# Attention heads 0 to 2: the four logit tiles in one run in four banks, the transposes of the probabilities in pairs

## The chip, the cores and the metric

The kernel runs on one core of one Trainium2 chip. The metric is the device time of one execution in microseconds (us). The engines are named as in the profile: PE is TensorE (matmuls and transposes), PEld its weight loads, DVE is VectorE, ACT is ScalarE, POOL is GpSimd, SP is SyncE, which issues the DMAs.

## The reference

One decoder layer over 512 tokens of width 1024. The part around the change is its sparse attention, four heads of width 128:

```python
(hq, hf, hi, hg, aq, ak, av, iq, ik, iw) = jnp.split(h @ w_in[layer], split_points, axis=-1)
o_hg = hgrn2_mixer(hq, hf, hi, hg, ...)          
q = partial_rope(q.reshape(B, T, ATT_HEADS, ATT_HEAD_DIM), positions)
k = partial_rope(k.reshape(B, T, ATT_HEADS, ATT_HEAD_DIM), positions)
score = jnp.einsum('bqh,bqhs->bqs', wi, jax.nn.relu(s))     # indexer, causal
_, idx = lax.top_k(score, topk)                             # 128 keys for each query
logits = jnp.einsum('bqhd,bqkhd->bhqk', qb, ks) * scale
p = jax.nn.softmax(jnp.where(valid, logits, -inf))
o = jnp.einsum('bhqk,bqkhd->bqhd', p, vs)
y = jnp.concatenate([o_hg, o_att], axis=-1) @ w_out[layer]
```

Before it stand the modulated norm and the input projection, beside it the gated linear recurrence (HGRN2), and behind it the output projection and the SwiGLU feed-forward layer. The kernel doesn't gather the selected keys: it adds a bias of about -1e30 to the logits of the keys that were not selected.

## The kernel before

The program is written engine by engine; the order on every engine is the order of the code, and semaphores tie the engines together. Weights and activations are split in a high and a low part, and each product with a weight is three matmuls (high by high, high by low, low by high). `w_raw` is the weight that a DMA loads, ACT makes `w_hi` of it (`split_hi`, L527), and DVE `w_lo` (`split_lo`, L1013). There are eight PSUM banks of 128 x 512, `ps[0]` to `ps[7]`.

**PE** (from L2007). `att_body(h, first)` treats attention head h; h = 0 is written out (`first`), h = 1 and 2 are a loop on the engine, and head 3 is code of its own (from L2073), between pieces of the output projection. While head h is attended, PE projects the q, k and v of head h + 1: 24 steps of three matmuls (`fill`, `att_project`, L1671), eight steps each for q, k and v, into banks 1, 0 and 1. Between them stand, for the four row tiles t = 0 to 3 of head h (128 queries each, t + 1 blocks of 128 keys):

- `logits(h, t, bank)`, L2009: one fp32 matmul of 128 x 128(t + 1), which the profile shows as two instructions. The logits 0 and 1 go to banks 2 and 3, the logits 2 and 3 to banks 2 and 3 again, once DVE has read them (`te.wait_ge(lg_ok, ...)`).
- `turn_v`, L2014: the four transposes of v into bank 6.
- `turn_probs(h, t, bank)`, L2022: t + 1 transposes of the probabilities into bank 4 or 5, after `p_ok`, which DVE raises.
- `values(h, t, 7)`, L2029: the product with the values, into bank 7.

The order is: steps 0 to 4, wait for the rotation (`a_rope`), logits 0 and 1, `turn_v`, (head 0: two steps), logits 2 and 3, steps up to 7, then three steps ahead of each `turn_probs`, four steps, `values`.

**ACT** (`att_body`, L793 to L826) goes in this order for each head: it waits for `turn_v` (`v_mm`) and copies bank 6 to `av_tok` (L802); exponentials of tiles 0 and 1 (L813); the copy of the next head's q out of its bank (`att_raw`, L718) and `split_hi`; the exponential of tile 2; the transposed probabilities of tile 0 out of their bank (`put_pt`, L806); the exponential of tile 3; `put_pt(1)`; `att_raw` of k; `put_pt(2)`, `put_pt(3)`; `att_raw` of v.

**DVE** (`att_body`, L1396 to L1456) goes in this order: `split_lo`; for each tile the logits plus bias out of the bank into `probs[t]` with the row maximum (L1414), the negated maximum (L1418), and then `normalise(t - 1)` (L1402, L1404), which waits for the exponential of tile t - 1; after tile 2 two `add_sum` (L1104, work for later modulation) and a `split_lo`; `normalise(3)`; two more `add_sum`, `split_lo`, and the rotation of the next head's q and k (`att_rotate`, L1386 to L1391), which raises `a_rope`; the copy of bank 7 (L1455).

Names in the trace: `res` holds aq, ak, av, av_tok, the probabilities and their transposes; `mx` and `nmx` are row maxima, `rs` and `ri` row sums and their inverses. `oln_ok` counts ACT's reads of bank 4 at the end of the recurrence's heads.

Of the kernel before, what the change touches and what calls it, by code (L numbers as in the profile page):

```python
# [7 lines left out]
P = 128  # L8
D_MODEL = 1024
SEQ = 512  # L10
HG_HEADS = 4
ATT_HEADS = 4
# [8 lines left out]
TT = SEQ // P  # L21
# [48 lines left out]
def build(nc, x, c, positions, w_ada, b_ada, norm_post_mix, norm_post_ffn, w_in, w_out, w_ffn_in, w_ffn_out, small_rows,  # L70
# [5 lines left out]
    with ctx:  # L76
# [78 lines left out]
        probs = [part(res, p_off[t], P * (t + 1)) for t in range(TT)]  # L155
# [31 lines left out]
        ps = [ctx.enter_context(nc.psum_tensor(f"ps{b}", [P, SEQ], f32)) for b in range(8)]  # L187
# [334 lines left out]
        def _(sc):  # L522
# [272 lines left out]
            def att_body(h, last):  # L795
                if last:
                    for k in range(4):
                        split_x_hi(k)
                        if k in (1, 2):
                            split_hi(1 + k, U_OUT[1 + k], G_OUT)  # L800
                sc.wait_ge(v_mm, h + 1)
                sc.activation(av_tok, ps[6][:, :], ACT.Copy).then_inc(v_ok, 1)  # L802

                def put_pt(t):
                    sc.wait_ge(pt_mm, h * 4 + (t + 1))
                    sc.activation(pt.rearrange("p (s t) -> p s t", s=TT)[:, 0:t + 1, t * P:(t + 1) * P],  # L806
                                  ps[7 - t % 2 if last else 4 + t % 2][:, 0:P * (t + 1)].rearrange(
                                      "p (s t) -> p s t", s=t + 1),
                                  ACT.Copy).then_inc(pt_ok, 1)

                for t in range(TT):
                    sc.wait_ge(nm_ok, h * 4 + (t + 1))
                    sc.activation(probs[t], probs[t], ACT.Exp, bias=nmx[:, t:t + 1], scale=float(HEAD ** -0.5),  # L813
                                  accum_out=rs[:, t:t + 1]).then_inc(exp_ok, 1)
                    if t == 1 and not last:
                        att_raw(h + 1, (0,))
                    if t >= 2:
                        put_pt(t - 2)
                    if last and t == 2:
                        sc.activation(ones_r[:, :], ones[:, :], ACT.Copy).then_inc(ones_ok, 1)  # L820
                        sc.wait_ge(sum_used, KT)
                        sc.activation(first_hi[:, :], sum_gate_mix, ACT.Copy).then_inc(gate_hi_ok, 1)
                if not last:
                    att_raw(h + 1, (1,))
                put_pt(2)
                put_pt(3)  # L826
                if not last:
                    att_raw(h + 1, (2,))
# [172 lines left out]
        def _(ve):  # L1001
            V = nc.vector
# [390 lines left out]
            def att_body(h, first, last):  # L1393
                sums = ((0, 1, 2, 3), range(4, 10), range(10, 14), (14, 15))[h]
                if first:
                    ve.wait_ge(sin_ok, 4)  # L1396
                    att_rotate(0)
                    ve.wait_ge(top_rep, HG_HEADS * 12)

                def normalise(t):  # L1400
                    ve.wait_ge(exp_ok, h * 4 + (t + 1))
                    V.reciprocal(ri[:, t:t + 1], rs[:, t:t + 1]).then_inc(ri_ok, 1)  # L1402
                    ve.wait_ge(ri_ok, h * 4 + (t + 1))
                    V.tensor_scalar(probs[t], probs[t], ri[:, t:t + 1], None, ALU.mult).then_inc(p_ok, 1)  # L1404

                if not (first or last):
                    split_lo(h * 3 + (G_ATT + 4), 1)
                for t in range(TT):
                    if first and t:
                        V.tensor_scalar(bias_t[t], sc_t[t], TAKEN / 2, NEG, ALU.is_gt, ALU.mult).then_inc(bias_ok, 1)  # L1410
                        ve.wait_ge(bias_ok, t)

                    ve.wait_ge(lg_mm, h * 4 + (t + 1))
                    V.tensor_tensor_reduce(out=probs[t], in0=ps[(4 if last else 2) + t % 2][:, 0:P * (t + 1)],  # L1414
                                           in1=bias_t[t], scale=1.0, scalar=TAKEN, op0=ALU.add, op1=ALU.max,
                                           accum_out=mx[:, t:t + 1]).then_inc(lg_ok, 1)
                    ve.wait_ge(lg_ok, h * 4 + (t + 1))
                    V.tensor_scalar(nmx[:, t:t + 1], mx[:, t:t + 1], float(-HEAD ** -0.5), None,  # L1418
                                    ALU.mult).then_inc(nm_ok, 1)
                    if t:  # L1420
                        normalise(t - 1)
                    if first and t == 1:
                        split_lo(G_ATT + 4, 1)
                    if last and t < 3:
                        split_x_lo(t + 1)
                        split_lo(G_OUT + 1 + t, 1 + t)
                    if not last and t == 2:
                        add_sum(sums[0])
                        add_sum(sums[1])
                        split_lo(h * 3 + (G_ATT + 5), 2)  # L1430
                normalise(TT - 1)
                if first:
                    head_tail(HG_HEADS - 1)
                if not last:
                    add_sum(sums[2])
                    add_sum(sums[3])
                    split_lo(h * 3 + (G_ATT + 6), 0)
                    att_rotate(h + 1)
                    for i in sums[4:]:
                        add_sum(i)  # L1440
                if h == ATT_HEADS - 2:
                    split_x_lo(0)
                if last:
                    ve.wait_ge(gate_hi_ok, 1)
                    V.tensor_tensor(first_lo[:, :], sum_gate_mix, first_hi[:, :].bitcast(f32),
                                    ALU.subtract).then_inc(gate_lo_ok, 1)
                    add_sum(sums[0])
                    add_sum(sums[1])
                    ve.wait_ge(post_loaded, 16)
                    for b in range(2):  # L1450
                        ve.wait_ge(gate_mm, b + 1)
                        V.tensor_tensor(gate_mix[:, b * SEQ:(b + 1) * SEQ], ps[(5, 7)[b]][:, :],
                                        gate_mix[:, b * SEQ:(b + 1) * SEQ], ALU.mult).then_inc(gate_ok, 1)
                ve.wait_ge(pv_mm, h * 4 + 4)
                V.tensor_copy(mix[:, (HG_HEADS + h) * SEQ:(HG_HEADS + h + 1) * SEQ],  # L1455
                              ps[4 if last else 7][:, :]).then_inc(att_out, 1)  # L1456
# [205 lines left out]
        def _(te):  # L1662
# [187 lines left out]
            for unit in (2, 3, 4):  # L1850
                k, first = START_TILES[unit][0] - 1, 4 * int(unit == 2)
# [152 lines left out]
            hg_body(HG_HEADS - 1, True)  # L2004

            def logits(h, t, bank):
                if t >= 2:  # L2007
                    te.wait_ge(lg_ok, h * 4 + (t - 1))
                mm(ps[bank][:, 0:P * (t + 1)], aq[:, t * P:(t + 1) * P], ak[:, 0:P * (t + 1)], start=True,  # L2009
                   stop=True).then_inc(lg_mm, 1)  # L2010
# [6 lines left out]
            def turn_probs(h, t, bank):  # L2017
                te.wait_ge(p_ok, h * 4 + (t + 1))
                if t >= 2:
                    te.wait_ge(pt_ok, h * 4 + (t - 1))  # L2020
                for s in range(t + 1):
                    last_mm = nc.tensor.transpose(ps[bank][:, s * P:(s + 1) * P], probs[t][:, s * P:(s + 1) * P],  # L2022
                                                  ident[:, :])
                last_mm.then_inc(pt_mm, 1)
# [8 lines left out]
            def att_body(h, first):  # L2033
                def fill(start, end):

                    att_project(h + 1, start, end)

                if not first:
                    te.wait_ge(v_ok, h)
                te.wait_ge(a_raw, h * 3 + 3)  # L2040
                fill(0, 5)
                te.wait_ge(a_rope, h * 2 + 2)
                logits(h, 0, 2)
                logits(h, 1, 3)
                turn_v()
                if first:
                    fill(5, 7)
                logits(h, 2, 2)
                logits(h, 3, 3)
                fill(7 if first else 5, 8)  # L2050
                for t in range(TT):
                    fill(8 + 3 * t, 11 + 3 * t)
                    if t == 1:
                        te.wait_ge(v_ok, h + 1)
                    turn_probs(h, t, 4 + t % 2)
                fill(20, 24)
                if first:
                    te.wait_ge(hg_out, HG_HEADS)
                for t in range(TT):
                    values(h, t, 7)  # L2060
# [237 lines left out]
```

## Time and profile before

| | |
|---|---|
| time, median of 3 runs | 693.54 us (693.03 to 693.98) |
| the profiled execution: its own time | 693.87 us |
| its span | 692.1 us |
| PE busy | 680.6 us, 98% of the span |
| DVE busy | 555.7 us, 80% |
| ACT busy | 334.5 us, 48% |
| DMA, mean rate | 128 GB/s |
| granted clock of PE, mean | 1.0 |

The span goes from the first to the last instruction that the profile shows; the time of the execution also holds what lies around it. Times in the views count from the span's start. A line of a timeline gives the start, the time up to the end of the last of the merged instructions, the engine, the line of the kernel, the operation and its count; what stands in square brackets is the engine's idle time ahead of it and what ended it. The attention heads 0 to 2 take the stretch from about 214 to 284 us.

### The profile page before, as it was taken

The page shows a single profiled execution, that of the slowest core. Times are in us where ns is not written, and L with a number is a line of the kernel's source. Part 1 is how long each engine was busy: PE and PEld are TensorE (multiplying, and loading weights), DVE is VectorE, ACT ScalarE, POOL GpSimd, SP SyncE. Part 2 cuts the span into 40 slices and gives each one's busy share as a digit, 9 for nine tenths or more (in the row PEclk, how much of TensorE's full clock was granted, in tenths as well). Part 3 has the DMA queues.
Part 4 walks back from the last instruction along what each step waited for, and adds up shares of the span by engine and source line. Part 5 has one row for each costly group of instructions (what it writes and reads, how often), then busy time and mean ns, then how long its engine had stood idle before and what let it go on. Part 6 is the DMA issues. An engine that isn't in the chain of part 4 may idle for free.

```text
span 692.1 us, 12998 instructions
## 1 busy us (share of the span) xinstructions
PE 680.6 (98%) x4640; PEld 567.9 (82%) x4640; DVE 555.7 (80%) x938; ACT 334.5 (48%) x569; POOL 135.1 (20%) x109
## 2 busy tenths in 40 slices
PE   7999999999999999999999999999999999999996
PEld 6566677777777878888788999999999998888885
DVE  3777999898898988988977799999999985344444
ACT  7357653545445344545753455555556551121123
POOL 4000000000000000000005567666766700000000
PEclk9999999999999999999999999999999999999999
DMA  9963222232224656568163255344433443322202
GB/s 274 357 207 95 61 63 62 75 107 61 62 62 119 217 183 217 179 230 254 31 183 91 71 145 149 115 130 130 131 110 114 122 131 126 109 92 91 61 10 112
DMA packets 97707, 88.92 MB, mean 128 GB/s; under 512 B 2735, under 2 KB 86787, under 8 KB 97670
## 3 DMA queue, kind: packets, MB, share of 16 engines
q1 hardware_dynamic: 97670, 88.44, 42.1%
q8 instruction: 21, 0.34, 0.2%
q14 instruction: 16, 0.13, 0.1%
HBM read 86.33 MB, written 2.10 MB: 128 GB/s over the span
## 4 chain that ended last, share of the span: by engine, by line
PE 62%; DVE 4%; issue 1%; ACT 0%; DVEq 0%; ACTq 0%
PE ps L2196 26%; PE ps L1690 17%; PE ps L1671 7%; PE ps L1708 6%; DVE rope L1104 1%; PE ps L2009 1%; DVE w_lo L1013 1%; PE ps L2029 1%; PE ps L2167 1%; PE ps L2174 1%; PE ps L1729 1%; PE ps L2169 1%; DVE act L1386 0%; DVE res L1391 0%; DVE act L1389 0%
## 5 line engine op out<-in xcount | busy, mean ns | idle before, releaser
L1671 PE MATMUL ps<-h_hl,w_hi 128*128 128x512 f32 x544 | 176.5, 405 | 0.0
L527 ACT ACTIVATE w_hi<-w_raw 128x1024 fp32r<-128x1024 f32 (+1 forms) x72 | 72.7, 1015 | 98.7 <-PE ps L1690 83.9
L1671 PEld LDWEIGHTS ps<-h_hl,w_hi 128*128 128x128 f32 x544 | 97.7, 188 | 24.6 <-issue 5.5
L1671 PE MATMUL ps<-h_hl,w_lo 128*128 128x512 f32 x272 | 106.6, 392 | 0.0
L2196 PE MATMUL ps<-h_hl,w_hi 128*128 128x256 f32 x576 | 104.5, 283 | 0.0
L2196 PEld LDWEIGHTS ps<-h_hl,w_hi 128*128 128x128 f32 x576 | 90.0, 192 | 0.2
L1013 DVE TENSOR_TENSOR w_lo<-w_raw,w_hi 128x1024 fp32r<-128x1024 f32 (+1 forms) x72 | 84.9, 1184 | 5.6 <-ACT w_hi L527 5.1
L1690 PE MATMUL ps<-w_hi,ht_hl 128*128 128x512 f32 x288 | 88.9, 389 | 0.0
L2196 PE MATMUL ps<-h_hl,w_lo 128*128 128x256 f32 x288 | 81.5, 283 | 0.0
L2196 PE MATMUL ps<-ht_hl,w_hi 128*128 128x256 f32 x432 | 78.5, 283 | 0.0
L2196 PEld LDWEIGHTS ps<-ht_hl,w_hi 128*128 128x128 f32 x432 | 67.4, 192 | 0.0
L1690 PEld LDWEIGHTS ps<-w_hi,ht_hl 128*128 128x128 f32 x288 | 54.1, 188 | 11.2
L2196 PE MATMUL ps<-ht_hl,w_lo 128*128 128x256 f32 x216 | 61.1, 283 | 0.0
L1671 PEld LDWEIGHTS ps<-h_hl,w_lo 128*128 128x128 f32 x272 | 51.1, 188 | 11.3
L1690 PE MATMUL ps<-w_lo,ht_hl 128*128 128x512 f32 x144 | 56.0, 389 | 0.0
L2196 PEld LDWEIGHTS ps<-h_hl,w_lo 128*128 128x128 f32 x288 | 55.3, 192 | 0.0
L1541 DVE TENSOR_TENSOR w_lo<-mix,w_hi 128x1024 fp32r<-128x1024 f32 x36 | 50.5, 1403 | 5.4 <-ACT w_hi L924 5.2
L1541 DVE TENSOR_TENSOR w_lo<-w_raw,w_hi 128x1024 fp32r<-128x1024 f32 (+1 forms) x36 | 53.2, 1478 | 0.0
L1550 DVE CAST ht_hl<-act 128x512 fp32r (+1 forms) x22 | 9.4, 426 | 53.7 <-PE ps L1690 53.2
L924 ACT ACTIVATE w_hi<-mix 128x1024 fp32r<-128x1024 f32 x36 | 38.0, 1056 | 22.8 <-PE ps L2196 18.9
L503 POOL TENSOR_TENSOR mix<-w_raw 128x512 f32<-128x512 f32 x18 | 23.8, 1324 | 117.1 <-DMA w_raw<-in_w_ffn_in 73.5
L491 POOL MEMSET res<- 128x1024 f32 x1 | 1.0, 962 | 230.1 <-DVE mix L1455 230.1
(310 smaller groups left out, 1260.2 us busy)
## 6 DMA issues: line engine op xcount, KB each, us to landing
w_raw<-in_w_ffn_in SPq DMA_DIRECT2D x44, 512.0 KB, 4.6
w_raw<-in_w_in SPq DMA_DIRECT2D x28, 512.0 KB, 4.0
w_raw<-in_w_ffn_out SPq DMA_DIRECT2D x22, 512.0 KB, 3.6
act<-in_w_ada SPq DMA_DIRECT2D x12, 512.0 KB, 8.4
adaw<-in_w_ada SPq DMA_DIRECT2D x6, 1024.0 KB, 5.2
act<-in_w_ada SPq DMA_DIRECT2D x6, 1024.0 KB, 5.2
res<-in_x SPq DMA_DIRECT2D x8, 512.0 KB, 5.6
w_raw<-in_w_out SPq DMA_DIRECT2D x8, 512.0 KB, 5.4
```

The source lines that it names most:

```text
L503: pool.tensor_tensor(s1, up_w[:, 0:QUART], up_w[:, QUART:2 * QUART], ALU.add).then_inc(s_ok, 1)
L527: sc.activation(w_hi[slot][:, 0:n], w_raw[slot][:, 0:n], ACT.Copy).then_inc(hi_ok, 1)
L924: sc.activation(w_hi[u][:, 0:src.shape[1]], src, ACT.Copy).then_inc(hi_ok, 1)
L1013: V.tensor_tensor(w_lo[slot][:, 0:n], w_raw[slot][:, 0:n], w_hi[slot][:, 0:n].bitcast(f32), ALU.subtract).then_inc(lo_ok, 1)
L1104: V.scalar_tensor_tensor(out=total, in0=w, scalar=silu, in1=total, op0=ALU.mult, op1=ALU.add).then_inc(sum_used, 1)
L1541: V.tensor_tensor(w_lo[u][:, 0:n], src, w_hi[u][:, 0:n].bitcast(f32), ALU.subtract).then_inc(lo_ok, 1)
L1550: V.tensor_copy(ht_hi[:, at], act[:, ds(k * SEQ, SEQ)]).then_inc(xs_hi, 1)
L1671: last = mm(ps[bank][0:rows, :], a, b, start=(k == 0 and n == 0), stop=(k == KT - 1 and n == 2))
L1690: last = mm(ps[2 * t + b][:, :], a, w, start=(first and n == 0), stop=False)
L1708: last = mm(ps[2 * t + b][:, :], a, w, start=False, stop=(n == 3 and m == 2))
L1729: return nc.tensor.transpose(ps[k][:, t * P:(t + 1) * P], xn[:, t * D_MODEL + k * P:t * D_MODEL + (k + 1) * P], ident[:, :])
L2196: last_mm = mm(ps[bank][:, 0:HALF], a, b, start=(start and k == 0 and n == 0), stop=(k == 3 and n == 2), skip_group_check=not start)
```

## The change

The four logit tiles of a head come right behind one another, into banks 2, 3, 4 and 5, without a wait for DVE between them, and `turn_v` comes behind them. The steps 5 to 12 follow in one run, then the transposes of the probabilities of tiles 0 and 1, the steps 13 to 18, the transposes of tiles 2 and 3, and the steps 19 to 23. The transposes go to banks 4, 2, 3 and 4. Ahead of those of tile 0 PE waits until DVE has read the logits of tile 2 out of bank 4; in head 0 it waits, ahead of the logits, for ACT's last read of bank 4 (`oln_ok`). Head 3 keeps its order and banks. DVE and ACT change only the bank that they read.

```diff
@@ -804,7 +804,7 @@
                 def put_pt(t):
                     sc.wait_ge(pt_mm, h * 4 + (t + 1))
                     sc.activation(pt.rearrange("p (s t) -> p s t", s=TT)[:, 0:t + 1, t * P:(t + 1) * P],
-                                  ps[7 - t % 2 if last else 4 + t % 2][:, 0:P * (t + 1)].rearrange(
+                                  ps[7 - t % 2 if last else (4, 2, 3, 4)[t]][:, 0:P * (t + 1)].rearrange(
                                       "p (s t) -> p s t", s=t + 1),
                                   ACT.Copy).then_inc(pt_ok, 1)
 
@@ -1411,7 +1411,7 @@
                         ve.wait_ge(bias_ok, t)
 
                     ve.wait_ge(lg_mm, h * 4 + (t + 1))
-                    V.tensor_tensor_reduce(out=probs[t], in0=ps[(4 if last else 2) + t % 2][:, 0:P * (t + 1)],
+                    V.tensor_tensor_reduce(out=probs[t], in0=ps[4 + t % 2 if last else 2 + t][:, 0:P * (t + 1)],
                                            in1=bias_t[t], scale=1.0, scalar=TAKEN, op0=ALU.add, op1=ALU.max,
                                            accum_out=mx[:, t:t + 1]).then_inc(lg_ok, 1)
                     ve.wait_ge(lg_ok, h * 4 + (t + 1))
@@ -2004,7 +2004,7 @@
             hg_body(HG_HEADS - 1, True)
 
             def logits(h, t, bank):
-                if t >= 2:
+                if bank > 3 and isinstance(h, int) and h == ATT_HEADS - 1 and t >= 2:
                     te.wait_ge(lg_ok, h * 4 + (t - 1))
                 mm(ps[bank][:, 0:P * (t + 1)], aq[:, t * P:(t + 1) * P], ak[:, 0:P * (t + 1)], start=True,
                    stop=True).then_inc(lg_mm, 1)
@@ -2040,20 +2040,20 @@
                 te.wait_ge(a_raw, h * 3 + 3)
                 fill(0, 5)
                 te.wait_ge(a_rope, h * 2 + 2)
-                logits(h, 0, 2)
-                logits(h, 1, 3)
+                if first:
+                    te.wait_ge(oln_ok, HG_HEADS)
+                for t in range(TT):
+                    logits(h, t, 2 + t)
                 turn_v()
-                if first:
-                    fill(5, 7)
-                logits(h, 2, 2)
-                logits(h, 3, 3)
-                fill(7 if first else 5, 8)
-                for t in range(TT):
-                    fill(8 + 3 * t, 11 + 3 * t)
-                    if t == 1:
-                        te.wait_ge(v_ok, h + 1)
-                    turn_probs(h, t, 4 + t % 2)
-                fill(20, 24)
+                fill(5, 13)
+                te.wait_ge(lg_ok, h * 4 + 3)
+                turn_probs(h, 0, 4)
+                te.wait_ge(v_ok, h + 1)
+                turn_probs(h, 1, 2)
+                fill(13, 19)
+                turn_probs(h, 2, 3)
+                turn_probs(h, 3, 4)
+                fill(19, 24)
                 if first:
                     te.wait_ge(hg_out, HG_HEADS)
                 for t in range(TT):
```

The first place is PE in the loop of heads 1 and 2, from the end of the first five steps (L1671) on: logits (L2009) and transposes of v (L2014), with the semaphores that each row waits for. Before:

```order
L2042 ISA
L2009 MATMUL ps<-res 128x128 [waits a_rope]
L2009 MATMUL ps<-res 128x256
L2014 MATMUL ps<-ident,res 128x128 x4
L2008 ISA
L2009 MATMUL ps<-res 128x384 [waits lg_ok]
L2008 REGISTER_ALU
L2009 MATMUL ps<-res 128x512 [waits lg_ok]
L1671 MATMUL ps<-h_hl,w_hi 128x512 x2
```

And now:

```order
L2042 ISA
L2009 MATMUL ps<-res 128x128 [waits a_rope]
L2009 MATMUL ps<-res 128x256
L2009 MATMUL ps<-res 128x384
L2009 MATMUL ps<-res 128x512
L2014 MATMUL ps<-ident,res 128x128 x4
L1671 MATMUL ps<-h_hl,w_hi 128x512 x2
```

The logits of 384 and 512 columns have moved ahead of the four transposes of v, and their two waits for DVE are gone.

The second place is PE in the same loop, at the transposes of the probabilities (L2022) of tiles 0 and 1, as it is now:

```order
L2049 ISA
L2018 REGISTER_ALU [waits lg_ok]
L2022 MATMUL ps<-ident,res 128x128 [waits p_ok]
L2018 REGISTER_ALU [waits v_ok]
L2022 MATMUL ps<-ident,res 128x128 [waits p_ok]
L2022 MATMUL ps<-ident,res 128x128
L1671 MATMUL ps<-h_hl,w_hi 128x512 x2
```

Three steps stood between the first of these transposes and the other two; those steps are now split between the places ahead of the pair and behind it.

The third place is ACT in head 0, whose order is the same before and after: the copy of the transposed v (L802) stands ahead of the first exponential (L813).

```order
L802 ACTIVATE res<-ps 128x512 [waits v_mm]
L813 ACTIVATE res,rs<-res,nmx 128x128 [waits nm_ok]
L813 ACTIVATE res,rs<-res,nmx 128x256 [waits nm_ok]
L718 ACTIVATE res<-ps 128x512 [waits group_done]
L527 ACTIVATE w_hi<-w_raw 128x1024 [waits group_done,w_loaded2]
```

Nothing moved here; ACT's copy follows wherever PE's transposes of v go.

## Rows read from the trace of the kernel before

**Rows 1.** The page of the profile: the span, busy time by engine, the chain of waits by engine.

```profile
span 692.1 us, 12998 instructions
...
PE 680.6 (98%) x4640; PEld 567.9 (82%) x4640; DVE 555.7 (80%) x938; ACT 334.5 (48%) x569; POOL 135.1 (20%) x109
...
PE 62%; DVE 4%; issue 1%; ACT 0%; DVEq 0%; ACTq 0%
```

**Rows 2.** Stretches of heads 0, 1, 2: length, busy us by engine, granted clock, DMA.

```profile
214.30:237.08 22.78, 22.78 (x115) 18.42 (x115) 20.30 (x44) 12.34 (x23) 0.00 (x0) 1.00 0.58 176
237.08:260.77 23.69, 22.98 (x117) 18.36 (x116) 21.56 (x45) 9.37 (x19) 0.00 (x0) 1.00 0.64 206
260.77:283.61 22.84, 22.70 (x118) 18.50 (x116) 20.72 (x42) 9.93 (x21) 0.00 (x0) 1.00 0.72 253
```

**Rows 3.** Timeline of PE, head 1: start, us, line, operation, [idle <-releaser].

```profile
240.35 0.39 PE L1671 MATMUL ps<-h_hl,w_lo 128*128 128x512 f32 x1
240.87 0.92 PE L2009 MATMUL ps<-res 128*128 128x128 f32 x4
241.62 0.60 PE L2014 MATMUL ps<-ident,res 128*128 128x128 f32 x4
242.81 1.77 PE L2009 MATMUL ps<-res 128*128 128x384 f32 x4 [0.58 <-DVE mx L1414]
...
244.88 0.39 PE L1671 MATMUL ps<-h_hl,w_lo 128*128 128x512 f32 x1
```

**Rows 4.** Timeline of PE, head 2, then the first logits of head 3.

```profile
264.27 0.82 PE L2009 MATMUL ps<-res 128*128 128x128 f32 x4
264.93 0.60 PE L2014 MATMUL ps<-ident,res 128*128 128x128 f32 x4
265.36 1.67 PE L2009 MATMUL ps<-res 128*128 128x384 f32 x4
266.47 1.02 PE L1671 MATMUL ps<-h_hl,w_hi 128*128 128x512 f32 x2
267.33 0.40 PE L1671 MATMUL ps<-h_hl,w_lo 128*128 128x512 f32 x1
...
281.08 2.39 PE L2029 MATMUL ps<-res 128*128 128x128 f32 x20
283.61 0.89 PE L2009 MATMUL ps<-res 128*128 128x128 f32 x4
```

**Rows 5.** Timeline of DVE, where heads 0 to 2 wait, and the last rotations.

```profile
220.40 0.16 DVE L1402 RECIPROCAL ri<-rs 128x1 f32<-128x1 f32 x1 [0.40 <-ACT res L813]
...
229.60 0.49 DVE L1404 TENSOR_SCALAR res<-res,ri 128x512 f32<-128x512 f32 x1
...
240.13 0.68 DVE L1391 TENSOR_TENSOR res<-act 32x512 f32<-32x512 f32 x1
...
243.50 0.16 DVE L1402 RECIPROCAL ri<-rs 128x1 f32<-128x1 f32 x1
...
248.27 1.23 DVE L1013 TENSOR_TENSOR w_lo<-w_raw,w_hi 128x1024 fp32r<-128x1024 f32 x1 [0.57 <-ACT w_hi L527]
...
265.60 0.15 DVE L1418 TENSOR_SCALAR nmx<-mx 128x1 f32<-128x1 f32 x1
266.57 0.17 DVE L1402 RECIPROCAL ri<-rs 128x1 f32<-128x1 f32 x1 [0.82 <-ACT res L813]
...
282.78 0.68 DVE L1391 TENSOR_TENSOR res<-act 32x512 f32<-32x512 f32 x1
```

**Rows 6.** Timeline of ACT: the copy of the values, head 2.

```profile
265.56 0.60 ACT L802 ACTIVATE res<-ps 128x512 f32<-128x512 f32 x1 [5.20 <-PE ps L2014]
```

**Rows 7.** Timeline of PE, head 0: the transposes of tile 2.

```profile
229.34 0.49 PE L2022 MATMUL ps<-ident,res 128*128 128x128 f32 x3
```

**Rows 8.** Timeline of PE at the start of the kernel: two runs of 128x128 transposes.

```profile
2.45 4.11 PE L1756 MATMUL ps<-ident 128*128 128x128 f32 x20
7.43 1.09 PE L1774 MATMUL ps<-ident,act 128*128 128x128 f32 x8 [0.87 <-DVE act L1065]
```

## The prediction

> **What bounds the kernel now.** I read the page first. PE is busy for 680.6 of 692.1 us, and the chain that ended last lies on PE for the most part [rows 1]. So the kernel is bound by PE's instructions in their order, and a change of order can gain only the time in which PE waits. The second view is the three stretches of heads 0 to 2, each from its first projection step to the next head's (the last up to head 3's first logits): 22.78, 23.69 and 22.84 us, with the same work in each [rows 2]. The reader should see that head 1 is 0.9 us longer than the other two.
>
> PE's timeline shows where. Head 1's last projection matmul starts at 240.35 and takes about 0.23, so it is through at 240.58; the logits start at 240.87, 0.29 late. The rotation on DVE ends at 240.13 + 0.68 = 240.81 and is what they wait for. The four transposes of v start at 241.62 and take 0.43 (in head 2, 265.36 - 264.93), so PE is free at 242.05, and the next logits start at 242.81: 0.76 of waiting, for DVE to read the first logits out of bank 2 [rows 3, 4, 5]. In head 2 that wait is not there: 265.36 - 264.93 is the transposes alone. But before head 3 there is one for DVE again: the values start at 281.08 and would end at 283.31 (20 instructions at about 0.11), the rotation ends at 282.78 + 0.68 = 283.46, and the logits start at 283.61 [rows 4, 5]. So DVE's rotation of the next head is the second bound here, 0.3 us behind PE.
>
> The third view is DVE's own waits. They are short, and the one that matters is at L1402, the inverse of the row sum of tile 0. It waits for ACT's first exponential: 0.40 in head 0, nothing in head 1, 0.82 in head 2 [rows 5]. ACT can't do that exponential before it has copied v (L802), since that copy stands ahead of it in its program, and the copy waits for PE's transposes of v: in head 2, PE's logits start at 264.27, the copy at 265.56, L1402 at 266.57 [rows 4, 6]. That is a chain of 2.30 us from the first logits to L1402.
>
> **The change part by part.**
>
> *The wait for DVE between the logits goes.* It is worth 0.76 in head 1, and with it goes the slower start of the matmuls behind the wait: from 242.81 to the third projection matmul at 244.88 it is 2.07, and in head 2 from 265.36 to 267.33 it is 1.97, so 0.10 more. Together 0.86 [rows 3, 4]. Heads 0 and 2 have nothing to give back here.
>
> *The work itself stays.* Logits 0 and 1 take 0.66 (264.27 to 264.93), or 0.75 behind a wait (240.87 to 241.62). Logits 2 and 3 take 1.51: the 1.97 just named less two projection matmuls of 0.23 each. The transposes of the probabilities are the same ten at about 0.11 each. That they stand in pairs saves nothing that I can price, since two and three of them in a row already cost that much each, and the edit goes at 0. The register instructions in the loop are as many as before, within one or two; also 0.
>
> *The transposes of v come 1.51 us later.* They now stand behind logits 2 and 3. This is the costly part. Before, bank 6 was complete 0.43 us after logits 1; now the 896 columns of logits 2 and 3 lie between. ACT's copy, its first exponential, L1402, and with L1402 everything behind it on DVE, come later by as much as DVE was already waiting there.
>
> Head 0: DVE waited there, so all 1.51 arrive: L1402 from 220.40 to 221.91. Nothing on DVE up to the rotation of head 1 has slack that could take it up, since its other waits there (for the exponential of tile 3, for its own semaphores) hang on DVE's own earlier work. PE has one small wait more: the transposes of tile 2 started at 229.34 and now stand behind two more steps of 0.69, so those of tile 3 could start at 229.34 + 1.38 + 0.33 = 231.05, but the probabilities of tile 3 come at 229.60 + 0.49 + 1.51 = 231.60 [rows 5, 7]. That is 0.55 of waiting, and it is hidden: the first five steps of the next head are then through at 240.58 + 0.55 = 241.13, while the rotation ends at 240.81 + 1.51 = 242.32.
>
> Head 1: the logits start at 240.87 + 1.51 = 242.38, after 1.25 us of waiting. The four logits and the transposes of v take 0.75 + 1.51 + 0.43, so PE is at its next step at 245.07. Before it was there at 244.88 - 0.46 = 244.42. PE is **0.65 late** (1.51 - 0.86). L1402 comes 2.30 + 0.09 + 1.51 after the first logits, at 246.28, where it was at 243.50: DVE is 2.78 late. At 248.27 DVE had waited 0.57 for `w_hi`, which ACT makes when PE is through with q, at +0.65; that wait goes, and 2.21 stay [rows 3, 5]. From here to the rotation for head 2 there is room: it ended about 3 us ahead of its need.
>
> Head 2: the logits start at 264.27 + 0.65 = 264.92, and L1402 at 264.92 + 2.30 + 1.51 = 268.73, against 266.57. DVE itself was ready at 265.60 + 0.15 = 265.75, with its 2.21 at 267.96, so ACT still ends the wait. DVE is **2.16 late** [rows 5]. Nothing behind it takes that up, and the rotation for head 3 ends at 283.46 + 2.16 = 285.62. PE, which with its 0.65 is through with the values at 283.96, waits 1.8 us for it: head 3's first logits start at 283.61 + 2.16 = 285.77.
>
> From there on PE is busy without a gap to the end of the head, and DVE's work and PE's are shifted alike. So the sum is 2 x 1.51 - 0.86 = **+2.16 us**. The profiled execution took 693.87, 0.33 over the median; it would be 696.0, and the median of the runs goes from 693.54 to **695.7 us**.
>
> *Bounds of the 1.51.* The nearest rows below it: from the start of logits 2 to the first projection matmul, 266.47 - 265.36 = 1.11. Above it: the whole 1.77 of the merged row of head 1 [rows 3, 4]. With 1.11 the sum is 1.36, with 1.77 it is 2.68, so 694.9 to 696.2. I keep 1.51, since it is measured where PE ran without a break.
>
> **The rivals.** A difference of 0.2%, 1.4 us, is about what a measurement of this kernel can tell from none.
>
> *A, not slower: the banks decide.* If DVE were not held by the late copy of v, only the wait for the bank would go. Price: -0.86 in head 1, of which head 3's rotation leaves as much as DVE also gains; its 0.82 of waiting in head 2 would let it gain about that. It gives 692.7 us. For it speaks the 0.76 on PE [rows 3]; against it the 0.82 and 0.40 in which DVE sat at L1402 for ACT already [rows 5]. It decides if the exponential can start ahead of the copy, which ACT's order does not allow. The Trainium skill speaks for it (Perfetto Trace Analysis, Matmuls): independent groups of matmuls should rotate through the banks, so that their evacuation overlaps the next group. By that rule alone the sum would be -0.86; this trace agrees with it for one wait of three heads.
>
> *B, half of it absorbed.* Somewhere between head 0 and head 3 DVE has slack that I don't see, about as large as the 0.57 for `w_hi` or the 0.82 at L1402. Price: 0.6 to 1.4 less, so 694.3 to 695.1. Against it: these two waits are already counted, and PE's 0.65 plus 1.51 lead to the same 2.16 in head 2 whatever head 0 does.
>
> *C, slower still: PE's clock falls while PE waits.* The granted clock is 1.00, the 2.4 GHz level, in all three heads, with waits of up to 0.76 [rows 2, 3]. The longest wait would now be 1.8 us, and the trace has none as long with work on both sides. At the start of the kernel, from 2.45 us on, 20 transposes take 4.11 us, 0.205 each; eight later ones take 1.09 us with the drain of the last, at most 0.14 each, and those of heads 1 and 2 0.11 [rows 4, 8]. Such a stretch costs 20 x 0.095 = 1.9 us, and the time is 697.6. Against it: behind the 0.87 of waiting at 7.43 the transposes ran at the fast rate. The Trainium skill has the mechanism (TensorE: Matmul & The Clock Gate, What's actually happening): an array that has been idle gets half of its pulses.
>
> **How the numbers follow.** The forecast has 0.74, its bounds being 694.9 and 696.2. A has 0.05, B 0.12, C 0.06, and 0.03 is for something not named, on either side. The range of 694.5 to 696.6 takes in the forecast's bounds with the scatter of a median of three (about 0.4), and most of B; what it leaves out is A, C and the lower end of B. Slower by over 0.2% means over 694.9: nearly all of the forecast (0.71), C, and a little of B, together 0.80. Within 0.2%: 0.17. Faster by over 0.2%, under 692.1, would need more than A gives: 0.03.
>
> **What would show it.** Right, if in the changed kernel: L1402 of head 0 waits about 1.9 us for the exponential, and L1402 of head 1 over 1 us where it waited for nothing; head 1's logits wait over 1 us for the rotation (L1391) and none for `mx`; PE waits about half a microsecond in head 0 for tile 3's probabilities; head 3's first logits start at about 285.8, after 1.8 us without work on PE, and the lengths from there to the end are unchanged. Wrong, if the copy L802 comes less than 1.3 us later against the head's first logits, if head 3's logits start before 285, if the wait for `mx` is still there, or if PE's matmuls behind the long wait take twice their time.

## The result and the profile after

| | before | changed |
|---|---|---|
| median | 693.52 us (692.86 to 695.15, 14 runs) | 695.54 us (694.75 to 697.56, 14 runs) |
| profiled execution, its span | 693.87 us, 692.1 us | 697.08 us, 695.4 us |
| head 0's first logits to head 3's first logits | 65.61 us | 67.64 us |

The ratio is 1.0029, with a 95% interval of 1.002 to 1.0037: the change makes the kernel slower by 2.02 us. The page of the changed kernel answers to [rows 1]: PE is 1.8 us busier and the span 3.3 us longer.

```profile
span 695.4 us, 12998 instructions
...
PE 682.4 (98%) x4640; PEld 569.2 (82%) x4640; DVE 555.7 (80%) x938; ACT 334.0 (48%) x569; POOL 135.1 (19%) x109
...
PE 62%; DVE 3%; issue 1%; ACT 0%; DVEq 0%; ACTq 0%
```

The profiled execution is 3.21 us slower than that of before, the median only 2.02. Most of the difference lies at the start. Head 0's first logits begin at 219.14 in the changed kernel and at 218.00 before, though nothing ahead of them was changed. The stretches of the changed kernel show a lower granted clock there; the last line is the middle stretch of before:

```profile
15.00:18.00 3.00, 2.94 (x18) 1.77 (x15) 1.67 (x5) 1.78 (x3) 0.00 (x0) 1.00 1.12 324
18.00:21.00 3.00, 3.00 (x21) 1.38 (x20) 1.70 (x3) 0.69 (x1) 0.00 (x0) 0.56 1.07 350
21.00:24.00 3.00, 3.00 (x21) 2.01 (x13) 0.32 (x2) 1.20 (x2) 0.00 (x0) 0.87 1.10 364
...
18.00:21.00 3.00, 3.00 (x26) 1.54 (x24) 1.98 (x3) 1.08 (x2) 0.00 (x0) 1.00 1.07 348
```

The columns are those of [rows 2]. Before, all three stretches read 1.00. The shift varies from one execution to the next and is no part of the change: four of the ten traces of this document have such a dip of the clock, and among them is one whose PE code is that of before (e4). So I read every time below from the head 0 logits of its own trace, and the stretch up to the first logits of head 3 is the measure for each kernel. Behind it the two kernels are alike: PE's last matmul starts 402.95 us after head 3's first logits in the changed kernel (689.73 - 286.78) and 402.92 before. The parts add up: 1.14 at the start, 2.03 in the stretch and 0.03 behind it are 3.20 us.

PE's timeline of the changed kernel, against [rows 3, 4, 7]; the first five lines are head 0 up to its values, the next three run from the end of the five projection steps to the transposes of v of head 1, the next three are head 2, and the last is the start of head 3:

```profile
219.14 2.42 PE L2009 MATMUL ps<-res 128*128 128x128 f32 x8
221.40 0.60 PE L2014 MATMUL ps<-ident,res 128*128 128x128 f32 x4
...
224.72 0.74 PE L1671 MATMUL ps<-h_hl,w_hi 128*128 128x512 f32 x2 [0.64 <-DVE w_lo L1013]
...
232.75 0.93 PE L2022 MATMUL ps<-ident,res 128*128 128x128 f32 x7
...
236.96 2.39 PE L2029 MATMUL ps<-res 128*128 128x128 f32 x20
...
242.37 0.39 PE L1671 MATMUL ps<-h_hl,w_lo 128*128 128x512 f32 x1
243.50 2.42 PE L2009 MATMUL ps<-res 128*128 128x128 f32 x8 [0.73 <-DVE res L1391]
245.76 0.60 PE L2014 MATMUL ps<-ident,res 128*128 128x128 f32 x4
...
266.00 2.32 PE L2009 MATMUL ps<-res 128*128 128x128 f32 x8
268.15 0.60 PE L2014 MATMUL ps<-ident,res 128*128 128x128 f32 x4
...
282.74 2.39 PE L2029 MATMUL ps<-res 128*128 128x128 f32 x20
286.78 0.89 PE L2009 MATMUL ps<-res 128*128 128x128 f32 x4 [1.66 <-DVE res L1391]
```

The reader should see that the wait for `mx` in head 1 is gone, and that two larger waits for the rotation (L1391) stand in its place, ahead of head 1's logits (0.73 in the brackets) and of head 3's (1.66). The brackets count from the modelled end of the matmul before. DVE's waits at L1402, against [rows 5], in heads 0, 1 and 2, and the end of the last rotation:

```profile
223.05 0.16 DVE L1402 RECIPROCAL ri<-rs 128x1 f32<-128x1 f32 x1 [1.91 <-ACT res L813]
...
247.41 0.16 DVE L1402 RECIPROCAL ri<-rs 128x1 f32<-128x1 f32 x1 [1.30 <-ACT res L813]
...
269.80 0.16 DVE L1402 RECIPROCAL ri<-rs 128x1 f32<-128x1 f32 x1 [0.83 <-ACT res L813]
...
285.96 0.68 DVE L1391 TENSOR_TENSOR res<-act 32x512 f32<-32x512 f32 x1
```

And ACT, against [rows 6]: in head 0 the copy of v and the exponential behind it.

```profile
222.03 0.60 ACT L802 ACTIVATE res<-ps 128x512 f32<-128x512 f32 x1 [3.13 <-PE ps L2014]
222.53 0.39 ACT L813 ACTIVATE res<-res,nmx 128x128 f32<-128x128 f32 x1
```

In head 0 the wait at L1402 grew from 0.40 to 1.91 us, by the 1.51 of logits 2 and 3. In head 1 there was none and now it is 1.30. In head 2 it is 0.83, about as before (0.82). There the exponential comes 2.1 us later than before, by PE's 0.59 and the 1.51, and DVE is ready for it 2.07 us later (268.81 + 0.15 - 1.14 = 267.82 against 265.75).

### The profile page after: what moved, and what is told of

The parts are those of the page before. It is cut to its first block, busy times and chain, and to the rows that moved or that the text cites. A ratio compares the mean times of both kernels' runs of the same rounds, so it can differ in the third digit from the quotient of the medians.

```text
span 695.4 us, 12998 instructions
## 1 busy us (share of the span) xinstructions
PE 682.4 (98%) x4640; PEld 569.2 (82%) x4640; DVE 555.7 (80%) x938; ACT 334.0 (48%) x569; POOL 135.1 (19%) x109
## 4 chain that ended last, share of the span: by engine, by line
PE 62%; DVE 3%; issue 1%; ACT 0%; DVEq 0%; ACTq 0%
PE ps L2196 26%; PE ps L1690 17%; PE ps L1671 7%; PE ps L1708 6%; PE ps L2009 1%; PE ps L2029 1%; PE ps L2167 1%; DVE rope L1104 1%; PE ps L2174 1%; PE ps L1729 1%; PE ps L2169 1%; DVE w_lo L1013 0%; DVE act L1386 0%; DVE res L1391 0%; DVE act L1389 0%
## 5 line engine op out<-in xcount | busy, mean ns | idle before, releaser
L1671 PE MATMUL ps<-h_hl,w_hi 128*128 128x512 f32 x544 | 174.9, 403 | 0.6 <-DVE w_lo L1013 0.6
L1671 PEld LDWEIGHTS ps<-h_hl,w_hi 128*128 128x128 f32 x544 | 97.9, 188 | 24.4 <-issue 4.0
L1671 PE MATMUL ps<-h_hl,w_lo 128*128 128x512 f32 x272 | 106.5, 392 | 0.0
L1690 PE MATMUL ps<-w_hi,ht_hl 128*128 128x512 f32 x288 | 88.8, 389 | 0.0
L1690 PEld LDWEIGHTS ps<-w_hi,ht_hl 128*128 128x128 f32 x288 | 54.1, 188 | 11.1
L1671 PEld LDWEIGHTS ps<-h_hl,w_lo 128*128 128x128 f32 x272 | 51.1, 188 | 11.3
L1690 PE MATMUL ps<-w_lo,ht_hl 128*128 128x512 f32 x144 | 56.0, 389 | 0.0
```

The lines of the kernel that those rows point to most:

```text
L1671: last = mm(ps[bank][0:rows, :], a, b, start=(k == 0 and n == 0), stop=(k == KT - 1 and n == 2))
L1690: last = mm(ps[2 * t + b][:, :], a, w, start=(first and n == 0), stop=False)
```

## The experiments

The theory: ACT's copy of v stands ahead of its first exponential, so putting logits 2 and 3 ahead of the transposes of v makes DVE late, once in head 0 and again by head 2, and head 3 waits for it. The rivals: the four banks or the pairs of transposes cost the time, or the place of the copy has no effect.

Eight kernels were run. The comparison is with before on the same chip (median 693.45 for the first four, 693.69 for the last four). The "stretch" is that from head 0's first logits to head 3's in the profiled execution.

| kernel | median us | ratio to before (95%) | stretch us |
|---|---|---|---|
| before | 693.5 to 693.7 | | 65.61 |
| changed | 695.54 | 1.0029 (1.002 to 1.0037) | 67.64 |
| e1: changed, v's transposes early | 692.41 | 0.9984 (0.9975 to 0.9993) | 64.73 |
| e2: before, v's transposes late | 698.83 | 1.008 (1.0066 to 1.0093) | 71.26 |
| e3: changed, copy of v late on ACT | 692.56 | 0.9985 (0.9976 to 0.9994) | 64.24 |
| e4: before, copy of v late on ACT | 692.90 | 0.9989 (0.998 to 0.9998) | 65.07 |
| e5: before, pairs alone | 693.47 | 0.9995 (0.9987 to 1.0004) | 65.59 |
| e6: e1 and e3 together | 692.36 | 0.9983 (0.9974 to 0.9991) | 64.22 |
| e7: changed, v's transposes later still | 697.92 | 1.0065 (1.0052 to 1.0079) | 69.04 |
| e8: e3, and the rotation earlier on DVE | 692.69 | 0.9984 (0.9975 to 0.9992) | 63.94 |

**e1, the transposes of v back between the logits.**

```diff
-                for t in range(TT):
-                    logits(h, t, 2 + t)
-                turn_v()
+                logits(h, 0, 2)
+                logits(h, 1, 3)
+                turn_v()
+                logits(h, 2, 4)
+                logits(h, 3, 5)
                 fill(5, 13)
```

> The changed kernel with the transposes of v back between logits 1 and logits 2; four banks and pairs of transposes as changed. Late-copy theory (the copy of v stands ahead of ACT's first exponential, so logits 2 and 3 ahead of the transposes delay DVE by 1.5 us twice): the delay is gone and the missing wait for the bank pays 0.86 us in head 1, so 692.7 us against 693.5 before, and 2.9 less than the changed kernel. Rival, the four banks or the pairs of transposes cost the time: the kernel stays slower than before, at 695 or more. Waits: head 1's logits wait 0.3 us for the rotation, L1402 of head 0 waits 0.4 us.

Measured: 692.41 us, 1.0 under before and 3.1 under the changed kernel. The banks and the pairs are as in the change; only the place of four transposes differs, and the loss becomes a gain. PE's timeline of e1 at the first logits of heads 0, 1 and 3, and DVE's L1402 of head 0:

```profile
217.67 0.92 PE L2009 MATMUL ps<-res 128*128 128x128 f32 x4
...
240.52 0.92 PE L2009 MATMUL ps<-res 128*128 128x128 f32 x4 [0.21 <-DVE res L1391]
241.28 0.60 PE L2014 MATMUL ps<-ident,res 128*128 128x128 f32 x4
241.71 1.67 PE L2009 MATMUL ps<-res 128*128 128x384 f32 x4
...
282.40 0.89 PE L2009 MATMUL ps<-res 128*128 128x128 f32 x4 [0.24 <-DVE res L1391]
```

```profile
220.07 0.16 DVE L1402 RECIPROCAL ri<-rs 128x1 f32<-128x1 f32 x1 [0.41 <-ACT res L813]
```

Logits 2 of head 1 follow the transposes without a wait, at 241.71, which is what the banks are good for. The stretch is 0.88 shorter than before, where 0.86 was the price of that wait. The rival of costly banks or pairs is out.

**e2, the late transposes alone.** The wait for the bank, the banks 2 and 3 and the single transposes are those of before.

```diff
-                turn_v()
-                if first:
-                    fill(5, 7)
                 logits(h, 2, 2)
                 logits(h, 3, 3)
-                fill(7 if first else 5, 8)
+                turn_v()
+                fill(5, 8)
```

> The kernel before with one move alone: the transposes of v behind logits 3 in heads 0 to 2 (head 0's two steps between the logits go behind them); banks, waits and single transposes as before. Late-copy theory: slower by more than the changed kernel, since the wait for the bank is still there: about 2.0 us in head 0, as much again and more in heads 1 and 2, so about 4.5 us over before, 698.0 (bounds 696.5 and 699). Rival, the banks or the pairs cost the time: within 0.5 us of before, 693.5.

Measured: 698.83 us, 5.4 over before, in the stretch 5.65. The sign and the order of size are those of the theory, and the amount is 1 us over what I expected. The timeline of PE in e2 shows a wait that before did not have: in head 2 the logits wait 1.44 us for DVE's read of bank 2, where before they waited for nothing. Up to head 1's logits e2 loses 2.05 us (24.92 against 22.87), as expected; what the expectation had too small lies in heads 1 and 2, with 3.60 us against about 2.5.

```profile
244.15 1.77 PE L2009 MATMUL ps<-res 128*128 128x384 f32 x4 [1.02 <-DVE mx L1414]
...
268.31 1.77 PE L2009 MATMUL ps<-res 128*128 128x384 f32 x4 [1.44 <-DVE mx L1414]
...
288.55 0.89 PE L2009 MATMUL ps<-res 128*128 128x128 f32 x4 [1.60 <-DVE res L1391]
```

So the four banks did pay in the changed kernel: without them the same late transposes cost 5.65 instead of 2.03 (the pairs, the other difference, are worth nothing by e5).

**e3, the copy of v behind two exponentials on ACT.** PE and DVE are those of the change.

```diff
-                sc.wait_ge(v_mm, h + 1)
-                sc.activation(av_tok, ps[6][:, :], ACT.Copy).then_inc(v_ok, 1)
+                def copy_v():
+                    sc.wait_ge(v_mm, h + 1)
+                    sc.activation(av_tok, ps[6][:, :], ACT.Copy).then_inc(v_ok, 1)
+
+                if last:
+                    copy_v()
...
                     if t == 1 and not last:
+                        copy_v()
                         att_raw(h + 1, (0,))
```

> The changed kernel with one move on ACT alone: in heads 0 to 2 the copy of v stands behind the exponentials of tiles 0 and 1. PE and DVE as changed. Late-copy theory: the first exponential needs DVE's maximum only, L1402 no longer waits for the transposes of v, and PE's waits in heads 1 and 3 go (0.29 + 0.86 + 0.30), so 692.1 us. Rival, the late rotation has another cause on PE or in the banks: 695.5 as the changed kernel.

Measured: 692.56 us, 3.0 under the changed kernel, and a stretch of 64.24. PE's order is the costly one, and yet the cost is gone, so it ran through ACT's order and nothing else. ACT's timeline of e3 in head 0 (its lines stand later by 1 to 5: L803 is L802, L817 is L813):

```profile
220.54 0.40 ACT L817 ACTIVATE res<-res,nmx 128x128 f32<-128x128 f32 x1 [1.42 <-DVE nmx L1423]
...
222.26 0.60 ACT L803 ACTIVATE res<-ps 128x512 f32<-128x512 f32 x1 [0.26 <-PE ps L2019]
```

The exponential now waits for DVE's maximum and comes 1.72 us ahead of the copy. On one point the expectation was off: ahead of head 3 a wait of 0.24 us for the rotation is left; the 0.30 of before was expected to go.

**e4, the same move in the kernel before.**

> The kernel before with the same move on ACT alone; PE as before. Late-copy theory: DVE gains its waits at L1402 (0.4 in head 0, 0.8 in head 2), so the rotations come earlier: PE's 0.29 ahead of head 1's logits and 0.30 ahead of head 3's go, the 0.86 at the bank stays: 692.9 us. Rival, the first exponential is not held by the copy: 693.5, no change.

The edit is that of e3, made in the kernel before.

Measured: 692.90 us and a stretch of 65.07, 0.54 shorter than before. The first exponential was held by the copy in the kernel before too. The amount came out as expected, but not all of its parts. From head 0's first logits to head 1's, e4 is 0.29 us shorter (22.58 against 22.87), as expected. The 0.30 ahead of head 3's logits did not go: from head 2's to head 3's it is 19.33 us against 19.34. Instead 0.24 went between head 1's logits and head 2's (23.16 against 23.40), where nothing was expected. The wait for the bank in head 1 is shorter there, but still stands:

```profile
242.78 1.77 PE L2014 MATMUL ps<-res 128*128 128x384 f32 x4 [0.45 <-DVE mx L1419]
```

**e5, the pairs alone.**

```diff
-                for t in range(TT):
-                    fill(8 + 3 * t, 11 + 3 * t)
-                    if t == 1:
-                        te.wait_ge(v_ok, h + 1)
-                    turn_probs(h, t, 4 + t % 2)
-                fill(20, 24)
+                fill(8, 13)
+                turn_probs(h, 0, 4)
+                te.wait_ge(v_ok, h + 1)
+                turn_probs(h, 1, 5)
+                fill(13, 19)
+                turn_probs(h, 2, 4)
+                turn_probs(h, 3, 5)
+                fill(19, 24)
```

> The kernel before with the pairing alone: logits, banks 2 and 3, waits and the place of the transposes of v as before; the projection steps 8 to 12, the transposes of tiles 0 and 1, steps 13 to 18, those of tiles 2 and 3 (banks 4, 5, 4, 5), steps 19 to 23. Theory: ten transposes at 0.11 us wherever they stand, so no change: 693.5, and 65.6 us from head 0's first logits to head 3's as before. Rival, longer runs of one kind on PE pay: 0.3 us or more less in that stretch, 0.1 for each pair.

Measured: 693.47 us, a ratio of 0.9995 whose interval holds 1, and a stretch of 65.59 against 65.61. The pairs are worth nothing, as priced.

**e6, both remedies.** The edits of e1 and e3 together.

> The changed kernel with both moves: the transposes of v between logits 1 and 2, and on ACT the copy of v behind the exponentials of tiles 0 and 1. Late-copy theory: either move frees L1402, so both together give no more than the move on ACT alone: 64.2 us from head 0's first logits to head 3's, 692.3 us. Rival, the moves add up (0.9 and 1.4 us under before): 691.3 us.

Measured: 692.36 us and a stretch of 64.22, the same as e3's 64.24. The moves don't add up: once the exponential is free of the copy, the place of the transposes of v does not matter.

**e7, a larger dose.** The transposes of v stand one projection step later than in the change.

```diff
-                turn_v()
-                fill(5, 13)
+                fill(5, 6)
+                turn_v()
+                fill(6, 13)
```

> The changed kernel with the transposes of v one projection step (0.69 us) later still. Late-copy theory: the dose counts once in head 0 and once more by head 2, so 2 x 0.69 = 1.4 us more than the changed kernel: 69.0 us from head 0's first logits to head 3's, 696.9 us. Rival, a delay that counts once: 68.3 us and 696.2. Rival, no effect of the place of the copy: 67.6 us and 695.5.

Measured: a stretch of 69.04 us, 1.40 more than the changed kernel for 0.69 us of delay. The dose counts twice. The median missed: it is 697.92, 1.0 over what I expected, and its interval (from 697.3 on) does not hold 696.9. The profiled execution took 696.97 at a mean granted clock of 1.0 and was the fastest of six. Four of the others have 0.995 to 0.997, and a lower clock may be part of the excess; but the fifth took 697.64 at 0.999. There is no trace of these five, so the cause of the excess stays open. DVE and PE of e7 show the two delays and their end:

```profile
222.22 0.16 DVE L1402 RECIPROCAL ri<-rs 128x1 f32<-128x1 f32 x1 [2.61 <-ACT res L813]
...
247.28 0.16 DVE L1402 RECIPROCAL ri<-rs 128x1 f32<-128x1 f32 x1 [2.00 <-ACT res L813]
...
269.68 0.16 DVE L1402 RECIPROCAL ri<-rs 128x1 f32<-128x1 f32 x1 [0.83 <-ACT res L813]
```

```profile
286.65 0.89 PE L2009 MATMUL ps<-res 128*128 128x128 f32 x4 [2.33 <-DVE res L1391]
```

Each of the first two waits is 0.70 longer than in the changed kernel, and the third is the same.

**e8, the rotation ahead of an `add_sum`.** This is e3 with one more move, on DVE.

```diff
                     add_sum(sums[2])
-                    add_sum(sums[3])
                     split_lo(h * 3 + (G_ATT + 6), 0)
                     att_rotate(h + 1)
-                    for i in sums[4:]:
+                    for i in sums[3:]:
```

> The changed kernel with the copy of v behind two exponentials on ACT, and on DVE, in heads 0 to 2, the last add_sum ahead of the rotation moved behind it (1.3 us of DVE work). Theory: head 3's logits still wait 0.24 us for the rotation with the first move alone; now they don't, and PE runs from head 0 to head 3 without a wait: 64.0 us for that stretch, 692.1 us. Rival, PE is held by something else there: the wait stays or turns into one on another semaphore, 64.2 us.

Measured: 692.69 us and a stretch of 63.94, as the theory has it: the wait for the rotation is gone. But a new one stands right behind the stretch, for the low part of the output projection's input, which DVE now makes behind the moved `add_sum`. PE's timeline of e8 (L2013 is L2009, L1694 is L1690), and DVE's making of that part, which was at 283.39 before:

```profile
282.97 0.89 PE L2013 MATMUL ps<-res 128*128 128x128 f32 x4
...
284.77 0.47 PE L1694 MATMUL ps<-w_hi,h_hl 128*128 128x512 f32 x1 [0.47 <-DVE h_hl L1044]
...
283.95 0.67 DVE L1044 TENSOR_TENSOR h_hl<-mix,h_hl 128x512 fp32r<-128x512 f32 x1
```

Here the stretch alone misleads. It is the only kernel in which the time behind the stretch differs: from head 3's first logits to the last matmul it takes 403.65 us (686.62 - 282.97), where e3 takes 402.93 and all the others 402.92 to 402.97. The 0.30 us gained against e3 in the stretch are lost again by the 0.72 behind it. So the rival was right that the wait turns into one on another semaphore, and e8 gains nothing over e3.

e1, e3, e6 and e8 are about 1 us faster than before and 3 us faster than the changed kernel. Their intervals overlap, so none of them is shown to be the best. By the stretch, e3 and e6 are ahead of e1 by 0.5 us; the medians do not show it.

## Why the prediction was right

The forecast was 695.7 us, and the median is 695.54. In the stretch +2.16 was forecast and +2.03 measured. From one head's first logits to the next head's, the changed kernel takes 1.49 more, 0.90 less and 1.44 more than before; the forecast had 1.51, -0.86 and 1.51. The 0.13 that it had too much are spread over all three. Point by point, with the times of the changed kernel less the 1.14 of its start:

- *Logits 2 and 3 cost 1.51 between logits 1 and the transposes of v.* Measured: L1402 of head 0 waits 1.91, forecast 1.91. The copy of v (L802) comes 2.89 us after the first logits and came 1.39 after them before (219.39 - 218.00), so it is 1.50 later; the sign of being wrong was less than 1.3. e7 shows the same chain with another dose.
- *Head 1.* The logits start at 242.36, forecast 242.38; L1402 at 246.27, forecast 246.28.
- *Head 2.* The logits start at 264.86, forecast 264.92, so PE is 0.59 late and not 0.65. L1402 is at 268.66, forecast 268.73. The wait for `w_hi` was absorbed as priced.
- *Head 3.* The logits start at 285.64, forecast 285.77. PE has 1.81 us without work ahead of them (282.74 + 2.23 to 286.78), forecast 1.8.
- *The missing wait pays 0.86.* e1 shows 0.88 by itself, and e3 against e4, where the copy stands late in both, 0.83.
- *The pairs are worth 0.* e5 shows 0.02.

**One step was wrong.** In head 0 I had PE wait 0.55 us for the probabilities of tile 3. It doesn't: the seven transposes of tiles 2 and 3 run in one piece at 232.75. Instead PE waits 0.64 us at 224.72 for `w_lo` of the k weights, which DVE makes right behind L1402, and which PE needs at step 8. By this PE comes to the transposes of tile 3 late enough: their probabilities are there at 231.59 (232.24 + 0.49 - 1.14), forecast 231.60, and PE starts the seven transposes at 231.61, the three of tile 2 first. I had followed the late DVE to its later products and passed over the first. With the restart, PE reached its values at 235.82 (236.96 - 1.14), 0.89 later than before, where I had 0.55. It cost nothing in the sum, for the reason given in the prediction: the rotation came later still. So PE waited 0.9 us ahead of head 1's logits (from 242.37 + 0.23 to 243.50) and not 1.25; the sign of over 1 us that I gave for it did not come.

Rival A, that the banks decide, fell with the 1.91 at L1402; e1 and e3 are the kernels in which it comes true. B, a slack of 0.6 us or more that I had not seen, was not there: the forecast had 0.13 us too much. C, a falling clock behind the long wait, did not come either: the stretches with the wait ahead of head 3 and behind it read 1.00 in the changed kernel, and also in e7, with its 2.33 us of waiting:

```profile
284.00:287.00 3.00, 0.67 (x6) 0.50 (x6) 2.97 (x5) 3.00 (x5) 0.00 (x0) 1.00 0.57 229
287.00:290.00 3.00, 3.00 (x17) 2.51 (x17) 2.97 (x8) 1.60 (x5) 0.00 (x0) 1.00 0.00 0
```

## What to carry to other kernels

When instructions are moved on the busiest engine, look at the first thing that each other engine does with the moved result, and at what stands behind that in its program: here a copy that nobody needed soon held the exponential that DVE needed at once. A delay on a second engine can be paid more than once: here it was paid twice in three heads, so follow it over all rounds and not over one. More banks took away the wait that the profile showed, and paid 0.8 to 0.9 us once the order on ACT or PE let them. And where a stretch is the measure, look at what stands behind its end too: e8 won 0.3 us in the stretch and lost 0.7 behind it.

## What the runs showed of the hardware

I had not expected the granted clock to fall in a stretch in which PE was busy all the time. Between 18 and 21 us the changed kernel reads 0.56 with PE busy for 3.00 of 3.00 us, and the same stretch of before reads 1.00; a value between the two levels of 1.2 and 2.4 GHz means that PE had the lower one for part of it. PE had small matmuls there, with weights of 128 x 32 and of 128 x 72. The same sixteen matmuls take nearly twice the time; the first line is the changed kernel, the second before:

```profile
19.62 1.94 PE L1749 MATMUL ps<-act,silu_pad 128*32 128x256 f32 x16
...
19.37 1.07 PE L1749 MATMUL ps<-act,silu_pad 128*32 128x256 f32 x16
```

From the first matmul of L1813 to the first of L1827 the changed kernel takes 5.50 us (17.80 to 23.30) and before 4.11 (18.08 to 22.19), so the dip costs 1.39 us; up to there the changed kernel had been 0.28 us ahead of before. e8, e3 and e4 have it too, with 0.56, 0.55 and 0.53 between 18 and 21 us; before and the five other experiments read 1.00. In the four traces with the dip head 0's first logits start at 218.49 to 219.36 us, in the six without it at 217.29 to 218.18. So it moves a single execution by over half of what was to be measured here, and it is the reason to compare stretches and not whole spans of two profiled executions. Between 12 and 15 us, ahead of the dip, PE was busy for 2.94 to 3.00 of 3.00 us in the four and for 2.57 to 2.93 in the six; whether the one has to do with the other was not tried, and what decides whether the dip comes stays open.
